# Prompt attention with the values as weights in two column halves, the probabilities scaled before they are turned, and results that come out turned

## What is computed

```python
o_cmp = einsum('bgjti,bigd->btgjd', p_cmp, vcmp)          # 31 compressed blocks
o_sel = sel_attend(qg, ksb, vsb, idx, q_pos)              # with 512 tokens every block is chosen: causal attention
o_win = window_attend(qg, win_k, win_v, kw_pos, q_pos)    # window 512: causal attention too
o = g[..., 0:1] * o_cmp + g[..., 1:2] * o_sel + g[..., 2:3] * o_win
merged = gates[0] * (o_nsa @ w_br_nsa) + gates[1] * (o_gdn @ w_br_gdn) + gates[2] * (o_mem @ w_br_mem)
```

## Time and profile before

| | |
|---|---|
| median of 3 runs | 1635.58 us (1632.93 to 1638.93) |
| profiled execution | 1641.88 us, span 1640.1 us |
| TensorE products busy | 1461.0 us, 89% of the span |
| TensorE weight loads busy | 1342.2 us, 82% |
| VectorE busy | 871.5 us, 53% |
| ScalarE busy | 383.5 us, 23% |
| GpSimd busy | 82.5 us, 5% |
| mean granted TensorE clock | 0.925 |

### The profile page before, as it was taken

One profiled execution on the slowest core, in us unless ns is written; L12 is line 12 of the kernel. 1 busy time (PEld: TensorE's weight loads), 2 busy tenths in 40 slices (PEclk: granted clock), 3 DMA queues, 4 the chain that ended last, 5 costly groups with the idle time before them and its releaser, 6 DMA issues. The chain is left out here.

```text
span 1640.1 us, 27038 instructions
## 1 busy us (share of the span) xinstructions
PE 1461.0 (89%) x11343; PEld 1342.2 (82%) x11343; DVE 871.5 (53%) x1590; ACT 383.5 (23%) x891; POOL 82.5 (5%) x76
## 2 busy tenths in 40 slices
PE   6999899889968797989766689999989999999998
PEld 5778789789958586868543389899988999999998
DVE  3555256848633556564433355545746746465563
ACT  3543023222232344454221231000003101000000
POOL 1000001100011111111100000000000000000000
PEclk8999999999967697979678789999999999999999
DMA  9232035151321000010258442333240332323321
GB/s 351 72 116 97 13 95 184 56 201 57 119 53 53 0 1 1 2 52 2 100 190 312 175 124 79 107 99 95 91 156 26 104 104 78 103 80 99 93 88 53
DMA packets 115649, 159.03 MB, mean 97 GB/s; under 512 B 6040, under 2 KB 106840, under 8 KB 112779
## 3 DMA queue, kind: packets, MB, share of 16 engines
q1 hardware_dynamic: 111886, 122.76, 23.4%
q0 software_dynamic: 2304, 33.56, 5.1%
q10 hardware_dynamic: 1348, 1.12, 0.2%
HBM read 145.04 MB, written 16.66 MB: 99 GB/s over the span
## 5 line engine op out<-in xcount | busy, mean ns | idle before, releaser
L330 PE MATMUL ps<-uH,wh 128*128 128x260 f32 x576 | 165.9, 288 | 8.7 <-DVE wt L301 8.7
L330 PE MATMUL ps<-hH,wh 128*128 128x260 f32 x512 | 144.9, 283 | 2.6 <-DVE hT L301 2.6
L330 PE MATMUL ps<-mergedH,wh 128*128 128x260 f32 x512 | 145.7, 285 | 0.0
L330 PE MATMUL ps<-mergedT,wh 128*128 128x260 f32 x512 | 144.8, 283 | 0.0
L330 PE MATMUL ps<-hT,wh 128*128 128x260 f32 x512 | 144.8, 283 | 0.0
L330 PE MATMUL ps<-mergedH,wl 128*128 128x260 f32 x512 | 144.5, 282 | 0.0
L330 PE MATMUL ps<-hH,wl 128*128 128x260 f32 x512 | 144.5, 282 | 0.0
L457 PE MATMUL ps<-XT,w 128*128 128x256 f32 (+1 forms) x512 | 125.5, 386 | 6.3 <-DVE XT L520 6.0
L330 PEld LDWEIGHTS ps<-uH,wh 128*128 128x128 f32 x576 | 109.9, 191 | 13.6 <-DVE wt L301 8.9
L330 PE MATMUL ps<-uL,wh 128*128 128x260 f32 x384 | 109.1, 284 | 0.0
L330 PE MATMUL ps<-uH,tw 128*128 128x260 f32 x384 | 109.0, 284 | 0.0
(11 more groups left out here) (525 smaller groups left out, 3470.8 us busy)
## 6 DMA issues: line engine op xcount, KB each, us to landing
wt<-in_w_ff SPq DMA_DIRECT2D x32, 1024.0 KB, 5.4
wt<-in_w_in SPq DMA_DIRECT2D x15, 1024.0 KB, 5.7
tw<-in_w_in SPq DMA_DIRECT2D x12, 1024.0 KB, 5.3
ring<-in_cache_mem_kv SPq DMA_DIRECT2D x4, 2048.0 KB, 11.2
w<-in_cmp_w SPq DMA_DIRECT2D x8, 512.0 KB, 7.7
ring<-in_cache_win_kv SPq DMA_DIRECT2D x2, 2048.0 KB, 9.8
out_s_win<-in_cache_win_kv SPq DMA_DIRECT2D x1, 4088.0 KB
scratch_uhigh<-uH SPq DMA_DIRECT2D x1, 2080.0 KB
```

The costliest lines, as they stand in the source:

```text
L330: ins = pe.matmul(out, lhsT(i, c), rhs(j, c), start=(first and c == 0 and k == 0), stop=(last and c == chunks - 1 and k == 2))
```

## The change

In the pairs, units of branch 0 and 1 get a new step `scale` on VectorE between the exponential and the transposes: reciprocal of the sums, times the gate, then both heads' probabilities are multiplied by it in place. The transposes wait for it (`scaled`). In `values`, the 64 value columns are now the weights and the turned probabilities stream, head a writing to PSUM partitions a*64 to a*64+63, the two heads alternating. The result has the heads' columns on partitions and queries along the row; `finish` is one add of 128 columns. Memory units are as before. The compressed branch does the same: its gate is multiplied into the reciprocal ahead of the probabilities, its values products have values as weights in alternating halves, and the end is a copy. `proj[:, 0:4, 0:512]` now holds the mixer's result turned.

In the tail the four groups of transposes of branch 0 go; instead ScalarE copies and VectorE subtracts four slices of 512 columns straight from `proj`, and two waits ask for them.

```diff
@@ cmp_pe
-                        g = h // HPG
-                        ins = pe.matmul(ps[:, 0, h * HD:(h + 1) * HD], PTc[:, h, :], vc[:, g * HD:(g + 1) * HD], start=True, stop=True)
+                        g, lo = h // HPG, h % 2 * HD
+                        ins = pe.matmul(ps[lo:lo + HD, 0, h // 2 * P:(h // 2 + 1) * P], vc[:, g * HD:(g + 1) * HD], PTc[:, h, :], start=True, stop=True)
@@ pair_pe, turn
                     pe.wait_ge(p_ready, 2 * u + 2)
+                    if pairs[u][0] < 2:
+                        pe.wait_ge(scaled, scaled_before(u + 1))
@@ pair_pe, values
+                    if pairs[u][0] == 2:
...
+                    else:
+                        for c in range(n):
+                            for a in range(2):
+                                ins = pe.matmul(ps[a * HD:(a + 1) * HD, 3, 0:P], values_of(u, a)[c], PTb[u % 2][:, (a * n + c) * P:(a * n + c + 1) * P],
+                                                start=(c == 0), stop=(c == n - 1))
@@ cmp_dve
+                    ch.step(dve.tensor_tensor(cs[:, 1, :].rearrange("p (e h) -> p e h", e=2), cs[:, 1, :].rearrange("p (e h) -> p e h", e=2),
+                                              self.gate[:, qt, 0:3 * NH:3].rearrange("p (h e) -> p e h", e=2), ALU.mult))
...
-                    dve.tensor_tensor(proj[:, qt, 0:NH * HD].rearrange("p (h d) -> p h d", d=HD), ps[:, 0, :].rearrange("p (h d) -> p h d", d=HD), g0, ALU.mult).then_inc(c_done, 1)
+                    dve.tensor_copy(proj[:, 0:NH // 2, query(qt)], ps[:, 0, :].rearrange("p (i t) -> p i t", t=P)).then_inc(c_done, 1)
@@ pair_dve
+                def scale(u):
+                    br, qt, h = pairs[u]
+                    n = tiles_of(u) * P
+                    dve.wait_ge(p_ready, 2 * u + 2)
+                    ch.step(dve.reciprocal(rg[:, :], rs[:, u % 4, :]))
+                    ch.step(dve.tensor_tensor(rg[:, :], rg[:, :], self.gate[:, qt, 3 * h + 1 + br:3 * h + 5 + br:3], ALU.mult))
+                    for a in range(2):
+                        ins = dve.tensor_scalar(Pb[u % 2][:, a, 0:n], Pb[u % 2][:, a, 0:n], rg[:, a:a + 1], None, ALU.mult)
+                        if a == 0:
+                            ch.inc(ins)
+                    dve.wait_ge(ch.sem, ch.n)
+                    ins.then_inc(scaled, 1)
+
                 def finish(u):
                     br, qt, h = pairs[u]
                     dve.wait_ge(o_ready, u + 1)
+                    if br < 2:
+                        dst = proj[:, h // 2, query(qt)]
+                        dve.tensor_tensor(dst, ps[:, 3, 0:P], dst, ALU.add).then_inc(o_done, 1)
+                        return
...
+                    yield beat(u, 0.9)
+                    if u < NU and pairs[u][0] < 2:
+                        scale(u)
@@ stage_tail
-        turns = [(br, t) for br in range(3) for t in range(TT)] + [(0, TT), (2, TT), (1, TT)]
+        turns = [(br, t) for br in (1, 2) for t in range(TT)] + [(0, TT), (2, TT), (1, TT)]
...
+                def ready():
+                    for c in range(4):
+                        yield 2.0 + 2.2 * c
+                        act.copy(oH[:, 0, c, 0:SEQ], proj[:, c, 0:SEQ]).then_inc(nH_kept, 1)
...
+                def ready():
+                    for c in range(4):
+                        yield 2.7 + 2.2 * c
+                        dve.wait_ge(nH_kept, c + 1)
+                        dve.tensor_tensor(oL[:, 0, c, 0:SEQ], proj[:, c, 0:SEQ], oH.bitcast(F32)[:, 0, c, 0:SEQ], ALU.subtract).then_inc(nL_kept, 1)
```

More of the change, by code:

```diff
@@ L1529, in stage_prompt_mixers @@
         c_s, c_max, c_exp, c_p, c_t, c_tk, c_o, c_done, c_chain = (S("dc_" + x) for x in ("s", "max", "exp", "p", "t", "tk", "o", "done", "chain"))
-        s_ready, nmax, p_ready, pt_ready, pt_kept, o_ready, o_done, v_chain = (S("u_" + x) for x in (
-            "scores", "max", "exp", "turned", "kept", "out", "done", "chain"))
+        s_ready, nmax, p_ready, scaled, pt_ready, pt_kept, o_ready, o_done, v_chain = (S("u_" + x) for x in (
+            "scores", "max", "exp", "scaled", "turned", "kept", "out", "done", "chain"))
+        scaled_before = lambda u: sum(pairs[w][0] < 2 for w in range(u))
         hid0 = 2 * NB
@@ L1754, in cmp_dve @@
                     dve.wait_ge(c_o, qt + 1)
-                    g0 = self.gate[:, qt, 0:3 * NH:3].unsqueeze(2).broadcast_to([P, NH, HD])
-                    dve.tensor_tensor(proj[:, qt, 0:NH * HD].rearrange("p (h d) -> p h d", d=HD), ps[:, 0, :].rearrange("p (h d) -> p h d", d=HD), g0, ALU.mult).then_inc(c_done, 1)
+                    dve.tensor_copy(proj[:, 0:NH // 2, query(qt)], ps[:, 0, :].rearrange("p (i t) -> p i t", t=P)).then_inc(c_done, 1)
             def pair_dve(dve, ch):
@@ L2375, in stage_tail @@
         gated, taken, added = (S("m_" + x) for x in ("gated", "taken", "added"))
-        turned, oH_kept, oL_kept = (S("t_" + x) for x in ("turned", "oH_kept", "oL_kept"))
+        turned, oH_kept, oL_kept, nH_kept, nL_kept = (S("t_" + x) for x in ("turned", "oH_kept", "oL_kept", "nH_kept", "nL_kept"))
         s_in, stored = S("s_in"), S("s_stored")
@@ L2532, in sample @@
                     a.done(act.activation(so, so, ACT.Sqrt), "ro", 0)
-                by_key(dense(), turn(), sample())
+                by_key(dense(), turn(), ready(), sample())
             @block.vector
@@ L2654, in sample @@
                         v.done(dve.tensor_tensor(Si, Si, ps[:, 6 + i % 2, :].rearrange("p (s d) -> p s d", s=4), ALU.add), f"add{i}", 0)
-                by_key(splits(), dense(), turn(), sample())
+                by_key(splits(), dense(), turn(), ready(), sample())
                 dve.wait_ge(self.x_split.sem, self.x_split.n)
```

24 lines of the change are left out of this document (8 added, 16 removed).

## The result

The kernel after takes 1652.0 us (median of 4 runs, 1650.1 to 1653.6) against 1636.9 for the kernel before (4 runs). The ratio is 1.0082, 95% interval 1.0058 to 1.0106: slower by 13 us by the ratio and by 15 us by the two medians, clear of noise either way. The forecast was 1634, with a range up to 1651. The profiled execution took 1652.14 us (span 1650.4), 10.3 more than the one of before.

The account below looks back on a forecast made before the run. TensorE was taken as the bound of the pair stretch, though not a clean one; -12 - 2 - 1.9 + 10 + 2.5 + 2 = -1.4 us gave 1640.5 profiled, 1634 us as median, range 1618 to 1651.

Parts of the forecast that it names:

- Values products: Pair units on TensorE: values as weights, two heads overlapping in column halves, save 13.8 us, of which 12 counted.
- Compressed branch: Compressed branch's values products in the new form: -2 us, bounds -4 and 0.
- Tail: Start of the tail: four transposed groups, 16 transposes, go from TensorE: -1.9 us.
- Stops: Pair units: TensorE's turn waits for VectorE's new scaling step before it: +10 us.
- overlay: Scaling step laid over the kernel before's trace: 16 of 32 turns come too early, 17.2 us in sum.
- a stop often shortens the next one: Reason given for counting 10 us of new TensorE stops out of the 12.8 left.
- Shared port: Pair units: VectorE's scaling step meets GpSimd products on their common port, 4.2 us, +2.5 on the path, bounds 0 and 6.
- Clock: Pair stretch: new idle time on TensorE is followed by the half clock: +2 us, bounds 0 and 8.
- Slower: Rival, chance 0.20: VectorE's list becomes the bound in the pairs; +14 us, some 1649 us.
- Faster: Rival, chance 0.29: TensorE's list swallows the stops, costing 2 instead of 14.5 with port and clock; about -14, 1621 us.
- Doesn't do what it says: Rival, chance 0.05: heads' values products don't overlap, accumulating in one bank; +6 instead of -12, 1652 us.
- the transposes' waits of 10 us: Sign that the forecast is right: in the pair stretch, transposes wait for VectorE 10 us or so more.

Follow-up runs that it names:

- e1: Kernel after without its scaling step and TensorE's wait for it (row-sum division and gate of branches 0 and 1 left out): 1624.9 us, ratio 0.9913.
- e14: Kernel after with values products head by head and both heads written to the same column half: 1660.2 us, ratio 1.0135.
- e15: Kernel after with GpSimd's delta-rule mask products and output-gate products replaced by one-element fills: 1640.5 us, ratio 1.0005.
- e16: Kernel before with GpSimd's delta-rule mask products and output-gate products replaced by one-element fills: 1631.7 us, ratio 0.9961.
- e2: Kernel before with only the scaling step ahead of the turn and the one-addition finish put in: 1666.6 us, ratio 1.0162.
- e13: Kernel after with VectorE's scaling of unit u ahead of the finish of unit u-2 instead of behind it: 1656.1 us, ratio 1.0112.
- e10: Kernel after with the two multiplies of the probabilities moved from VectorE to ScalarE: 1659.5 us, ratio 1.0119.
- e9: Kernel after with the scaling moved behind the values products, applied to the turned result in the finish: 1627.6 us, ratio 0.994.
- e6: Kernel after with the gate as second scalar of the multiply, its separate gate product gone: 1646.6 us, ratio 1.0047.

## Why the prediction was wrong

Point by point, by its own steps:

- **Values products**, counted at -12 of 13.8: right. Their own records fell from 45.1 to 27.2 us, busy time in all by 14.3, and e1 puts the whole change without the scaling at -14 us, where the sum has -15.9 for values, compressed branch and tail. That the halves overlap is shown by e14, where the products cost 44.5 us in one half against 26.1 in two.
- **Compressed branch** -2: measured -0.9, inside its bounds. **Tail** -1.9: measured -1.0, over a stretch of 692 us. Both right in sign, half the size.
- **Stops**, +10: this is the step that failed first. With GpSimd's products out of both kernels (e15, e16) the idle time is 47.1 against 30.9: the term measured 16.2 us. The waits of these two kernels show where. At the turns they are 23.9 against 4.8, 19.1 more, and my overlay had 17.2: the overlay itself was right within 2 us. The waits that stood there anyway and went (for the finish 4.6, for delta products 2.8) make 7.4, where I took off 4.4; at unit 11, 5.12 us stand in place of 3.50, 1.6 net, where I had 1.4. But then I took off 2.8 more since "a stop often shortens the next one". That had no row behind it, and its sign was wrong: other waits grew by 4.2 us, those of the scores for the exponentials by 3.0 and of the delta products for g_qn by 1.2. Why the scores' waits grew is only partly known: in e1, with no scaling, they are up by 2.4 us already, and the scaling alone (e2) adds 1.3. The overlay was also laid on a timeline with the long values products. With them the step adds 20.0 us of idle time (e2), port included, and with the short ones 24.7 (e1 to the kernel after); no overlay on the kernel before could show that.
- **Shared port**, +2.5 with bounds 0 and 6: this is the second. The idle time gives 8.2 us, outside the bounds; the times, 6 to 8.5 with an interval that reaches down to 0, don't exclude them. I had 32 x 0.2 x 0.65 = 4.2 us of collisions and put 2.5 on the path. The trace has 10 steps of 32 that lose 0.85 us each, 8.5 in all, and nearly all of it shows as idle time. The chance was too low by its own numbers: a step of 1.1 us and a product of 1.26 overlap if the one starts within 2.4 us of the other, and 27 x 2.4 / 238.7 is 0.27, 8 or 9 steps. The rest of the error is the part put off the path. The Trainium skill, "SBUF — State Buffer", SBUF: two separate sides, calls the port pair an exclusive lock, which a VectorE instruction in a two-port mode takes too. The lengths of L1784 agree: 0.48 us in the mean for 256 columns, up to 1.44, and 0.35 without GpSimd's products. The alternative that only products with two tensors wait is shown wrong.
- **Clock**, +2: the granted clock of the pair stretch rose, from 0.87 to 0.90, against what I wrote. For the scaling alone the runs disagree: from e1 to the kernel after it fell by 0.01, with 4.5 us more of busy time, and from the kernel before to e2 it rose by 0.01. No size and no sign of this term is shown.

With 16.2 and 8.2 in place of 10 and 2.5 the sum is -1.4 + 6.2 + 5.7 = +10.5. The two profiled executions differ by 10.3, but that is partly luck, since 2.6 of it arose ahead of all changed code; the parts behind that differ by 7.7, and the busy time fell by 4 us more than the values and clock terms of the sum allow. The forecast failed by two sizes, stops and port. The rival "Slower" (stops 17, port 6, 1649 us) had sizes near the measured ones, at a chance of 0.20, but its mechanism, VectorE's list as the bound, is not what the runs show. VectorE is behind when the exponential ends, at 621.26 as in unit 31, but with the step ahead of the finish (e13) the idle time falls by 3.1 us only, with the multiplies off VectorE (e10) it doesn't fall, and e9 does 11 us more on VectorE than the kernel before at the same idle time. The rival "Faster" is out by the same rows: TensorE's list swallowed 12 of the 32 steps, where the overlay had 16. "Doesn't do what it says" is out by e14.

Of what was to show the steps, the transposes' waits of 10 us came to 30.7; that, beside 14 us less busy time, gives the sign of the result.

Open stays the exact share of the port (the times of two pairs and the idle time agree on 6 to 8.5 us, and the times' interval is as wide as that), why the waits of the scores grew, how much of the price is ScalarE's own list in e10, and why head by head products overlap as well as they do.

## What to carry to other kernels

When a step is laid over a trace by hand, take off what already stands idle in a row, and nothing on a general hope: here the overlay was right within 2 us of 19, and the discount without a row was wrong by 7. Lay it over a timeline that has the rest of the change in it: on one with the old, longer products the step cost 20.0 us of idle time, on one with the new ones 24.7. In this kernel the factor belonged behind the last product, where one result waits for it, and not ahead of the transposes, where TensorE's whole list does: ahead of the turn the scaling cost 27 us (38 us of VectorE's time against e1), behind the values 3 (30 us of it). When collisions on a shared resource are priced by chance, count with the lengths of both instructions, and leave none of them off the path if the step stands where the path runs.

## What the runs showed of the hardware

- Products with 64 weight columns and 128 moving columns that go to two column halves overlap: 26.1 us of TensorE for 304 records when alternating, 31.8 head by head, 44.5 when all go to one half.
- A VectorE product of 2 columns (0.16 us alone) took up to 1.27 us beside a GpSimd product of 1.26, and in-place multiplies with one tensor suffer the same way (256 columns: up to 1.44 us instead of 0.35).
- A second scalar operand made VectorE's in-place multiply 0.06 us longer at each of four sizes (0.285 to 0.345 us at 128 columns, 0.485 to 0.544 at 512; e6).
- A ScalarE in-place scaling of 512 columns took 0.72 us, VectorE's 0.48; at 128 columns 0.40 and 0.28.
